# Rows of the last two expert pairs scattered by token and read back by plain transfers

## What is computed

```python
g_w, g_idx = lax.top_k(g_probs, 1)                     # one group for each token
top_v, top_i = lax.top_k(in_group, TOP_K_IN_GROUP)     # two experts of it
hid = silu(x @ w_gate[e]) * (x @ w_up[e])
y = y + gate[token, e] * (hid @ w_down[e])             # added to the token's row
```

## Time and profile before

| what | value |
|---|---|
| median of 3 runs | 1228.85 us (1228.26 to 1231.77) |
| the profiled execution | 1228.01 us, its span 1226.2 us |
| layer 0's experts | about 400 to 650 us |
| layer 0's tail, to the first convolution products | 650 to 672.5 us |
| convolution, its projection and layer 1's router | 672.5 to about 937 us |
| layer 1's experts | about 937 to 1198 us |
| layer 1's tail, to the end | 1198 to 1226.2 us |

### The profile page before, as it was taken

The page is one execution under the profiler, slowest core; times in us unless marked ns, Lnnn a source line. Parts: engine busy times, 40 slices in busy tenths (PEclk is TensorE's granted clock), DMA queues, the critical chain, the costliest instruction groups (busy, mean ns, idle before and its releaser), DMA issues.

```text
span 1226.2 us, 14501 instructions
## 1 busy us (share of the span) xinstructions
PE 1059.7 (86%) x5296; PEld 617.6 (50%) x5296; DVE 496.4 (40%) x1061; ACT 296.5 (24%) x649; POOL 283.0 (23%) x286
## 2 busy tenths in 40 slices
PE   5999999999997898787884998998996989878880
PEld 5777777776454433333323776764545333333330
DVE  3144444344346311111117698995457111111117
ACT  3223233223211111100003465555111111111003
POOL 2100000000000411111134398880002211110144
PEclk9999999999998899989987998999996999999895
DMA  8973123411725799999997294100018999999995
GB/s 274 376 242 111 68 69 94 136 58 59 282 102 203 277 418 420 419 413 420 420 393 234 58 359 120 34 1 26 35 37 318 406 419 419 388 421 420 420 379 190
DMA packets 109546, 304.79 MB, mean 249 GB/s; under 512 B 17359, under 2 KB 64591, under 8 KB 85782
## 3 DMA queue, kind: packets, MB, share of 16 engines
q1 hardware_dynamic: 87814, 253.95, 53.8%
q0 software_dynamic: 21520, 49.88, 11.1%
q10 hardware_dynamic: 160, 0.26, 0.1%
HBM read 274.94 MB, written 57.38 MB: 271 GB/s over the span
## 4 chain that ended last, share of the span: by engine, by line
PE 58%; DMA 21%; DVE 8%; issue 5%; POOL 3%; ACT 3%; another core or an unknown queue 1%; SPq 1%; POOLq 0%; DVEq 0%; ACTq 0%
DMA ring<-in_w_up 18%; PE bank L573 11%; PE bank L1280 10%; PE bank L472 7%; PE bank L1299 6%; PE bank L1610 5%; PE bank L600 4%; POOL ring L1784 3%; PE bank L623 2%; PE bank L639 2%; PE bank L664 2%; PE bank L380 2%; DMA work<-in_w_pw 2%; PE bank L1269 1%; PE bank L1006 1%
## 5 line engine op out<-in xcount | busy, mean ns | idle before, releaser
L1280 PE MATMUL bank<-ring,work 128*64 128x512 f32 x704 | 166.4, 628 | 31.5 <-DMA ring<-in_w_up 29.4
L1299 PE MATMUL bank<-ring,work 128*64 128x512 f32 x512 | 122.9, 624 | 26.3 <-DVE work L1318 22.1
L573 PE MATMUL bank<-arena,ring 128*128 128x288 f32 x512 | 131.9, 412 | 1.2 <-issue 1.2
L1610 PE MATMUL bank<-arena,work 128*128 128x256 f32 (+1 forms) x512 | 127.1, 411 | 6.3 <-DMA work<-in_w_pw 5.1
L1280 PEld LDWEIGHTS bank<-ring,work 128*64 128x64 f32 x704 | 58.1, 144 | 137.3 <-issue 135.9
L1314 DVE TENSOR_TENSOR work<-work,bank 128x256 f32<-128x256 f32 x32 | 13.5, 421 | 275.1 <-ACT work L1310 260.4
L1784 POOL TENSOR_TENSOR ring<-ring 128x576 f32<-128x576 f32 x76 | 107.2, 1410 | 41.4 <-ACT ring L1729 32.0
L1610 PEld LDWEIGHTS bank<-arena,work 128*128 128x128 f32 x512 | 98.3, 192 | 34.5 <-issue 7.1
L573 PEld LDWEIGHTS bank<-arena,ring 128*128 128x128 f32 x512 | 94.9, 190 | 33.8 <-issue 9.2
L472 PE MATMUL bank<-ring,arena 128*128 128x512 f32 x224 | 100.8, 604 | 2.6 <-ACT arena L1768 2.6
L1830 DVE SCALAR_TENSOR_TENSOR bank<-work,ring,bank 128x576 f32<-128x576 f32 x129 | 94.9, 817 | 0.0
(11 more groups left out here) (283 smaller groups left out, 1326.3 us busy)
## 6 DMA issues: line engine op xcount, KB each, us to landing
ring<-in_w_down SPq DMA_DIRECT2D x32, 2048.0 KB, 23.2
ring<-in_w_gate SPq DMA_DIRECT2D x20, 2048.0 KB
ring<-in_w_up SPq DMA_DIRECT2D x20, 2048.0 KB
arena<-in_w_gate SPq DMA_DIRECT2D x10, 2048.0 KB
arena<-in_w_up SPq DMA_DIRECT2D x8, 2048.0 KB
ring<-in_w_qkv SPq DMA_DIRECT2D x24, 512.0 KB, 6.1
y_sorted<-gain POOLq DMA_DIRECT2D x8, 1536.0 KB, 5.7
work<-in_w_pw SPq DMA_DIRECT2D x16, 512.0 KB, 5.4
```

Source lines behind the costliest of these rows:

```text
L573: mm = nc.tensor.matmul(bank[b][:, 0:HT], wa[s][:, w, c, :], xt[:, c, h * HT:(h + 1) * HT], start=c == 0, stop=c == C - 1)
L1280: mm = nc.tensor.matmul(bank[2 + s][rr, :], rows_t[:, c, rr], wgu[g][:, :, e, c, :], start=c == 0, stop=c == C - 1)
L1299: mm = nc.tensor.matmul(bank[5 + h][rr, :], hts[:, c, rr], wdn[s][:, e, c, h * HALF:(h + 1) * HALF], start=c == 0, stop=c == FC - 1)
L1610: mm = nc.tensor.matmul(bank[banks[h][w]][:, 0:end - at], wp[s][:, w, c, :], xt[:, c, at:end], start=c == 0, stop=c == C - 1)
```

## The change

The last two pairs scatter into a new DRAM table `y_tokens`, one row for each token (640 rows of 4 KB), at the token's own number `tok_at`. The table is zeroed once, at the start, by one more transfer of POOL. In the tail SyncE reads it back with five plain transfers of whole tiles, in place of POOL's five late gathers. In layer 1 a token without a late row can find layer 0's row there; its `late_gate` is 0. With the gathers go the five fills of `y_late` and the three VectorE instructions that made `late_slot`. SyncE's wait for `late_in[2]` ahead of the convolution's weights goes too. The early additions of tile 4 move on VectorE from ahead of the late ones to just ahead of tile 4's own late one.

```diff
@@ the start
             pool.dma_start(x_over.rearrange("(a p) d -> p a d", p=P), zeros(OPAIRS)).then_inc(zeros_in, 16)
+            pool.dma_start(y_tokens.rearrange("(a p) d -> p a d", p=P), zeros(TILES)).then_inc(zeros_in, 16)
@@ router_dve
             do(V.scalar_tensor_tensor(early_slot[:], late_is[:], float(ZERO_ROW), slot_f[:], ALU.mult, ALU.max))
-            do(V.scalar_tensor_tensor(far_f[:], late_is[:], -FAR, slot_f[:], ALU.mult, ALU.add))
-            do(V.tensor_tensor(far_f[:, 0, :], far_f[:, 0, :], far_f[:, 1, :], ALU.min))
-            do(V.tensor_scalar(late_slot[:], far_f[:, 0, :], FAR, None, ALU.add))
             dve.sem_inc(further_known, 1)
@@ experts_pool
             def rows_out(local):
-                pool.indirect_dma_start(y_sorted, bass.IndirectOffsetOnAxis(slot_at[:, local:local + 1], 0), ysb[local % 2],
-                                        None, bounds_check=EXPERTS * CAP - 1,
-                                        oob_is_err=False).then_inc(base.y_out[local % 2], 16)
+                if local < EARLY_PAIRS:
+                    to, at, end = y_sorted, slot_at, EXPERTS * CAP
+                else:
+                    to, at, end = y_tokens, tok_at, TOKENS
+                pool.indirect_dma_start(to, bass.IndirectOffsetOnAxis(at[:, local:local + 1], 0), ysb[local % 2],
+                                        None, bounds_check=end - 1, oob_is_err=False).then_inc(base.y_out[local % 2], 16)
...
                 if local == EARLY_PAIRS:
                     pool.wait_ge(base.gu_mm, i + 1)
-                    for j in range(TILES):
-                        steps.done(pool.memset(y_late[j], 0.0))
@@ the late rows
-        def late_pool(pool, l):
+        def late_sync(sp, l):
             for s in range(2):
-                pool.wait_ge(base.y_out[s], 16 * (EPAIRS // 2) * (l + 1) + 16)
+                sp.wait_ge(base.y_out[s], 16 * (EPAIRS // 2) * (l + 1) + 16)
             for j in range(TILES):
-                pool.indirect_dma_start(y_late[j][0:rows[j], :], None, y_sorted,
-                                        bass.IndirectOffsetOnAxis(late_slot[0:rows[j], j:j + 1], 0),
-                                        bounds_check=SLOTS - 1, oob_is_err=False).then_inc(late_in[j], 16)
+                sp.dma_start(y_late[j][0:rows[j], :], y_tokens[j * P:j * P + rows[j], :]).then_inc(late_in[j], 16)
@@ combine_dve
             r = rows[j]
+            if j == TILES - 1:
+                early_dve(dve, steps, l, j)
             dve.wait_ge(early_sum, TILES * l + j + 1)
@@ experts_dve
                 if local == EPAIRS - 1:
-                    for j in range(TILES):
+                    for j in range(TILES - 1):
                         early_dve(dve, steps, l, j)
@@ conv_first
-            sp.wait_ge(late_in[HALF_TILES - 1], 16)
             conv_load(sp, 0, 0)
```

More of the change, by code:

```diff
@@ L102, in encoder @@
         y_sorted = nc.dram_tensor("y_sorted", [SLOTS + P, D], F32).ap()
+        y_tokens = nc.dram_tensor("y_tokens", [TILES * P, D], F32).ap()
         x = sb("x", [P, TILES, D])
@@ L161, in encoder @@
         early_slot = sb("early_slot", [P, 2, TILES], I32)
-        late_slot = sb("late_slot", [P, TILES], I32)
         late_is = sb("late_is", [P, 2, TILES])
@@ L1153, in router_dve @@
             dve.sem_inc(further_known, 1)
-            FAR = float(2 * SLOTS)
             do(V.tensor_scalar(late_is[:], slot_f[:], float(EARLY_PAIRS * P), None, ALU.is_ge))
@@ L1192, in experts_pool @@
             if l == 0:
-                pool.wait_ge(zeros_in, 16 * (PAIRS + 1))
+                pool.wait_ge(zeros_in, 16 * (PAIRS + 2))
             pool.wait_ge(x_out, 16 * TILES * (l + 1))
@@ L1554, in experts_sync @@
                 conv_small(sp)
+            late_sync(sp, l)
         def conv_load(sp, cc, s):
@@ L1959, in _ @@
                 experts_pool(pool, steps, l)
-                late_pool(pool, l)
         @block.scalar
```

## The result

The change makes the kernel slower by less than half a per cent. Timed in 20 executions against 20 of the kernel before, it took 1232.12 us in the median (1227.32 to 1235.92) against 1228.72 (1225.33 to 1233.23), a ratio of 1.0027 with an interval of 1.0015 to 1.0039. The two intervals have 1.0015 to 1.0025 in common, 1.8 to 3.1 us. The profiled execution took 1233.10 us, with a span of 1231.4, 5.2 more than before.

A forecast was written before the change was run, and what follows sets the result against it. TensorE and weight transfers, untouched by the change, were taken to bound the kernel. Layer 0's tail -1.7 and layer 1's +0.2 sum to -1.5 us, from 1228.85 to 1227.3, with an 8-in-10 range of 1224.8 to 1230.3.

The forecast's parts named there:

- What bounds the kernel, and where the change acts: TensorE and weight transfers fill the chain, untouched; the change acts in two tails, the zeroing at the start and the router.
- the prediction's signs of being wrong: Load above 4.3 us, a changed span to layer 0's tail, or a convolution not shorter or later as its start.
- L: Both tails: time from pair 15's scatter landing to the first plain load's landing; taken as 3.5 us, bounds 2.6 and 3.9.
- only the first counts: Both tails: later loads follow at 1.26 us each, VectorE needs 1.28 per addition, so only the first load's landing matters.
- the zeroing: At the start: 2.62 MB, 6.3 us of transfers, hidden within 8.6 us of cover on SyncE's queue; costs nothing.
- Layer 0: -1.7 forecast: Layer 0's tail: first late addition moves from 661.55 to 659.81, -1.7 us, bounds -2.6 and -1.3; the convolution moves along.
- Layer 1, +0.2 forecast: Layer 1's tail: VectorE's late additions start at 1206.85 instead of 1206.64, moving the end +0.2 us, bounds -0.7 and +0.6.
- Rival 1: Both tails: plain loads late at 7.2 us, together +5.9, 1234.8; breaks even at 4.3 per load, sum 8.5; chance 0.11.
- Nothing in that stretch starts by anything but the tail: Argument against layer 0's gain being absorbed by the convolution or layer 1's weight stream (1229.1, chance 0.12).
- the moved additions: Layer 0's tail: tile 4's additions (2.56 us) delay the last norm about 1.5 us, cover 2.5; nothing, at most 0.5.
- the router's instructions: Router: three instructions fewer, 0.6 us a layer, not on the path because ScalarE's table load had waited 5.6 us; nothing.
- Rivals 2 and 3: Router instructions on the path, 1224.3, chance 0.11; zeroing delays SyncE's load beyond 8.6 us, holding up attention, 1232.9, chance 0.03.

The follow-up runs named there:

- change_kept: The change with 36 unread TensorE products behind pair 15's in layer 0, filling the idle time before the first late addition; ratio to the kernel before 1.0008 (0.9995 to 1.0021).
- wait_back: The change with SyncE's wait for the third late load put back ahead of the convolution's weights; ratio to the kernel before 1.0011 (0.9995 to 1.0027).
- order_back: The change with tile 4's early additions put back ahead of all late ones on VectorE; ratio to the kernel before 1.0020 (1.0005 to 1.0035).
- change_small: The change with TensorE's sixteen small transposes moved ahead of the wait for the first late addition; ratio to the kernel before 1.0024 (1.0012 to 1.0037).
- change_again: The same kernel as the change, run again for a second profile; ratio to the kernel before 1.0007 (0.9988 to 1.0025).
- more_running: The change with 12 in place of 6 unread products ahead of the first tile's transposes; ratio to the kernel before 1.0015 (1.0003 to 1.0026).
- layer1_only: Scatter by token, plain loads and new addition order in layer 1 only, layer 0 as before, table zeroed; ratio to the kernel before 1.0014 (0.9998 to 1.0030).
- first_alone: The change with SyncE waiting for the first late load before issuing the other four; ratio to the kernel before 1.0078 (1.0058 to 1.0098).
- zero_only: The kernel before with only the table and its one zeroing transfer added; ratio to the kernel before 1.0003 (0.9986 to 1.0019).
- gathers_ahead: The change with tile 4's two early gathers issued ahead of pair 15's scatter; ratio to the kernel before 1.0044 (1.0028 to 1.0059).
- ahead_order: The change with tile 4's gathers ahead of the scatter and its early additions back ahead of the late ones; ratio to the kernel before 1.0030 (1.0016 to 1.0045).
- gathers_behind: The change with tile 4's two early gathers held back until the first late load has landed; ratio to the kernel before 1.0015 (0.9999 to 1.0030).
- behind_kept: The change with tile 4's gathers behind the first late load and 34 unread products in TensorE's idle time; ratio to the kernel before 1.0006 (0.9992 to 1.0020).
- behind_running: The change with tile 4's gathers behind the first late load and 12 unread products ahead of the first transposes; ratio to the kernel before 0.9998 (0.9980 to 1.0016).
- before_kept: The kernel before with 44 unread TensorE products in its idle time in layer 0's tail; ratio to the kernel before 0.9987 (0.9972 to 1.0001).

## Why the prediction was wrong

**What bounds the kernel, and where the change acts: right.** Between the tails, from the first convolution product to pair 15's down products in layer 1, it was 521.5 us before (672.51 to 1193.98) and 523.6 in the change (672.78 to 1196.36), of which the first 24 products are 2.0. The tail of layer 0 itself began 1.3 us earlier in the change's profile (650.17 and 651.49), one of the prediction's signs of being wrong; but it was 651.49 in the change's second profile, and 649.7 to 653.6 over all of them, so it does not belong to the change.

**L: the step that failed.** The prediction took 3.5 us, from "between the shortest gather and that load", with 3.9 as the high end, and said "only the first counts". In the two profiles of the change the load took 4.72 and 4.44 in layer 0, 6.08 and 5.73 in layer 1, and 0.07 more with the way from the scatter's landing to the issue: above 4.3, as the prediction's own sign of being wrong asks. The size 3.5 is right for a load that meets nothing: 3.44 to 3.76 in the six kernels in which tile 4's gathers were ahead of it or behind it, siblings and all. It is wrong where these gathers are in flight. With 2 us between the issue of the second gather and that of the load it took 3.4 to 4.3, with about 1 us 4.4 to 4.9, with less 5.2 to 6.1, in each layer by itself too:

| run, layer | second gather issued | load issued | between | load took |
|---|---|---|---|---|
| change_kept, 0 | 653.13 | 655.35 | 2.22 | 3.40 |
| wait_back, 0 | 654.00 | 656.23 | 2.23 | 4.28 |
| change_kept, 1 | 1201.46 | 1203.51 | 2.05 | 4.12 |
| order_back, 0 | 654.58 | 655.64 | 1.06 | 4.94 |
| change_small, 0 | 653.93 | 654.99 | 1.06 | 4.37 |
| change_again, 0 | 655.15 | 656.20 | 1.05 | 4.44 |
| change, 0 | 653.80 | 654.82 | 1.02 | 4.72 |
| more_running, 0 | 653.17 | 654.07 | 0.90 | 4.83 |
| layer1_only, 1 | 1201.44 | 1202.28 | 0.84 | 5.40 |
| wait_back, 1 | 1204.17 | 1204.95 | 0.78 | 5.45 |
| more_running, 1 | 1200.29 | 1200.95 | 0.66 | 5.18 |
| change_small, 1 | 1200.40 | 1201.05 | 0.65 | 5.34 |
| first_alone, 0 | 657.14 | 657.67 | 0.53 | 5.34 |
| change, 1 | 1204.99 | 1205.22 | 0.23 | 6.08 |
| order_back, 1 | 1204.45 | 1204.68 | 0.23 | 6.06 |
| change_again, 1 | 1206.19 | 1206.41 | 0.22 | 5.73 |
| first_alone, 1 | 1208.12 | 1208.35 | 0.23 | 5.57 |

The Trainium skill, in "DMA: Bandwidth & Descriptors", section "Anatomy of one DMA", gives the fit behind the estimate of 3.2 us that the prediction quoted, for transfers that GpSimd issues; this load went by SyncE's queue, and undisturbed it took 3.4 to 3.8. The section "Queues, rings and completion order" of that page of the Trainium skill, on DMA engines that take turns between queues, would have the load share with POOL's gathers, and the rows above agree in direction (3.4 to 3.8 without them, up to 6.1 beside them). The prediction used that section for the zeroing only, where it was harmless, and not here, where it decided.

**Layer 0: -1.7 forecast.** To the first late addition it was -0.4, since the load took 1.2 us more than the term. Layer 1, +0.2 forecast, was +3.3 to the first late addition: on top of the 0.2 come 2.6 for the load, 0.5 between its landing and VectorE's start, and 0.1 ahead of its issue. Rival 1 was the right mechanism, with its place and its break-even: the two loads of the change add to 10.8 against its 8.5. I had given it 0.11, and of the two disturbers that I named ("the five loads go out together" and "tile 4's gathers are still in flight") only the second counts: with the gathers away the five together left the first at 3.4 to 3.8, and alone beside the gathers it took 5.3 and 5.6.

**"Nothing in that stretch starts by anything but the tail": TensorE's clock was left out.** From the first late addition to the end of the first 24 products it was 17.66 us before and 21.85 and 21.91 in the two profiles of the change, 4.2 more. Of these, 2.2 lie ahead of the products, in the transposes, and 2.0 in the products; TensorE ran there at the low clock until 676.8, before until 667.9. That was no term of the sum. With it the two profiles' difference closes: -0.4 + 4.2 in layer 0's tail, +3.5 in layer 1's, -0.7 in the two scatters and -1.3 for the earlier start are 5.3; the span grew by 5.2.

It is not the chance of one execution. In the kernel before, in the two others with its tail in layer 0 (zero_only, layer1_only) and in the two with the gathers ahead (gathers_ahead, ahead_order) the stretch took 17.6 to 17.7 us; in the change's two profiles, gathers_behind, wait_back, first_alone and order_back it took 19.3 to 22.8. The two with the gathers ahead have the plain loads as well, so it is not the loads as such. What it is worth in the median is open: the medians grew by 3.4 and 1.2 only, executions without a profile need not share the late return, and the kernels that mended half of it (change_kept) or nearly all (more_running) were not clearly faster.

**The terms at zero: right.** The zeroing (1.0003; in the change the slice was issued at 73.17 and landed 7.3 us later, at 80.5, TensorE's products of line L573 began at 82.12, before at 82.32), the scatter by token (4.58 and 3.16 against 4.82 and 3.6), the moved additions (order_back), the router's instructions (the first pair's down products began at 418.47, before at 418.55) and the fills. Rivals 2 and 3 did not happen.

**Still open.** Why gathers_behind and behind_kept, whose load is mended in both layers, are not under the kernel before is settled for their profiles only. Both spans are 1.9 us over before, and TensorE's stretch takes 4.2 and 2.2 us more in them, which the load and the scatter do not win back. In behind_running the late weights are the reason; in gathers_behind they were only close to late, landing at most 12.3 us after their issue, with the first product at 671.31. That the same holds in the median is not shown: 2 us of clock given back by the products of change_kept left no mark there. What TensorE must have done for the clock to come back was not found either.

## What to carry to other kernels

A load that replaces a late gather must be priced in the company that it will have: look at what every queue has in flight at the moment of its issue, and not only at its own queue. Here 3.5 us alone were up to 6.1 beside two gathers of 64 rows, and each attempt to clear the way (gathers earlier, gathers later) moved the wait to the next transfer: the scatter, then the convolution's weights. Moving a wait also moves when TensorE starts again, so compare the granted clock of the stretch behind it, and take a second profile before a term is built on it.

## What the runs showed of the hardware

- The scatter of 128 rows took 3.1 to 5.4 us where tile 4's gathers stood behind it (3.11 in layer 1 of zero_only, 5.35 in layer 0 of change_kept), and 7.42, 6.20, 8.00 and 5.37 with them ahead of it.
- After a fall in idle time the clock came back 3.4 to 24 us later (663.6 to 667.0 in before_kept, 654.1 to 678.0 in the change again), and it fell anew behind a wait of 1.21 us (order_back, at 672.8), though not behind the same wait in the kernel before. In the change TensorE worked at 1.2 GHz from 660.98 to 676.8, with but 1.2 us of waiting in one piece.
- 20 to 35 executions of one kernel spread over 8 to 10 us, and the spread goes with the mean granted clock: of 35 executions of the kernel before on one chip the span was 1222.7 us at a clock of 0.951 and 1231.7 at 0.940. With 12 executions against 35 the interval still reached some 2 us to each side (0.9988 to 1.0025), so a difference of 2 us takes more than that. Among the profiles the stretch from the end of the first 24 products to the issue of the last scatter took 517.6 to 521.6 us (before_kept and behind_running), whatever the tails; it was 520.5 in both the kernel before and the change.
